# Moving six row products of a recurrence head behind its last level and into its norm's waits

## The reference

```
h = x * (1 + scale1) + shift1
hq, hff, hfb, hi, hg, aq, ak, av, ga, gb = split(h @ w_in)
o_rec = rms_norm(scan_fwd(q, k_f, v, f_f) + scan_bwd(q, k_b, v, f_b)) * silu(hg)   # 8 heads of 128
o_att = attention(rms_norm(aq), rms_norm(ak), av)
x = layer_norm(alpha * x + gate1 * ((sig(ga) * (o_rec @ w_rec) + sig(gb) * (o_att @ w_att)) @ w_out))
# PEER mixer: 128 experts chosen for each token (8 heads x 16), rows of two large tables
a   = gelu(einsum('td,thkd->thk', h2, u_tab[expert]))
out = einsum('thk,thkd->td', gate * a, v_tab[expert])
x = layer_norm(alpha * x + gate2 * out)
```

## Time and profile before

| | |
|---|---|
| runs | 5602.97, 5605.55, 5614.87 us, median 5605.55 us |
| profiled execution, span | 5604.2 us (the page gives no time around the span; the median of the runs is 1.35 us more) |
| PE busy | 4557.5 us, 81% |
| DVE busy | 3712.8 us, 66% |
| POOL busy | 2184.8 us, 39% |
| ACT busy | 1424.7 us, 25% |
| row products of line 1879 | 256, 308.5 us busy, mean 1227 ns |
| latent recurrence heads | some 365 us in each of the two layers |

### The profile page before, as it was taken

One profiled execution on the slowest core, in us unless ns is written; L12 is line 12 of the kernel. 1 busy time (PEld: TensorE's weight loads), 2 busy tenths in 40 slices (PEclk: granted clock), 3 DMA queues, 4 the chain that ended last, 5 costly groups with the idle time before them and its releaser, 6 DMA issues. The chain is left out here.

```text
span 5604.2 us, 60591 instructions
## 1 busy us (share of the span) xinstructions
PE 4557.5 (81%) x17704; PEld 2520.6 (45%) x17704; DVE 3712.8 (66%) x7028; ACT 1424.7 (25%) x3646; POOL 2184.8 (39%) x1826
## 2 busy tenths in 40 slices
PE   7889988888676777777787999888795878777776
PEld 6556655646343322222265566556463433223222
DVE  2357768867788766754532677788677877677545
ACT  2112213411011333333321112134100113333333
POOL 0002124642656454455400121246336554444554
PEclk9999998999888999999999999989897989999999
DMA  7755336785989999999967543457869889999998
GB/s 267 266 184 194 122 131 219 255 331 215 384 318 346 421 419 418 418 421 416 383 225 275 197 163 117 175 191 254 330 243 365 326 311 421 421 419 411 421 421 345
DMA packets 296082, 1703.74 MB, mean 304 GB/s; under 512 B 33360, under 2 KB 43216, under 8 KB 175696
## 3 DMA queue, kind: packets, MB, share of 16 engines
q0 software_dynamic: 258048, 1342.29, 61.3%
q1 hardware_dynamic: 23712, 338.18, 15.8%
q10 hardware_dynamic: 14000, 19.42, 1.0%
HBM read 1694.52 MB, written 5.24 MB: 303 GB/s over the span
## 5 line engine op out<-in xcount | busy, mean ns | idle before, releaser
L368 POOL DMA_INDIRECT arena<-in_peer_uv,eidx x1024 | 1184.3, 1157 | 1458.7 <-POOLq L367 1195.4
L2151 DVE SCALAR_TENSOR_TENSOR arena<-arena 128x1024 f32<-128x1024 f32 x384 | 470.6, 1225 | 349.9 <-DMA arena<-in_peer_uv,eidx 338.4
L861 PE MATMUL banks<-arena 128*128 128x512 f32 x896 | 502.1, 643 | 237.7 <-PEq L1473 234.2
L411 POOL DMA_INDIRECT arena<-in_peer_uv,eidx x384 | 490.3, 1277 | 501.0 <-POOLq L410 475.7
L863 PE MATMUL banks<-arena 128*128 128x512 f32 x896 | 477.8, 616 | 0.0
L834 PE MATMUL banks<-ring,arena 128*128 128x512 f32 x864 | 383.7, 599 | 110.0 <-PEq L816 110.0
L463 ACT ACTIVATE arena<-arena 128x1 f32<-128x1 f32 (+1 forms) x772 | 156.9, 203 | 1035.4 <-ACTq L462 1033.6
L861 PEld LDWEIGHTS banks<-arena 128*128 128x128 f32 x896 | 155.3, 198 | 549.7 <-issue 549.2
L468 ACT ACTIVATE arena<-ident,arena 128x128 f32<-128x128 f32 x832 | 333.6, 401 | 234.7 <-ACTq L467 230.2
L2151 DVE SCALAR_TENSOR_TENSOR ring<-ring,arena 128x1024 f32<-128x1024 f32 x192 | 235.4, 1226 | 211.1 <-DMA ring<-in_peer_uv,eidx 209.9
L2161 DVE SCALAR_TENSOR_TENSOR arena<-arena 128x1024 f32<-128x1024 f32 x256 | 306.9, 1225 | 95.3 <-DMA arena<-in_peer_uv,eidx 80.8
(11 more groups left out here) (303 smaller groups left out, 7763.1 us busy)
## 6 DMA issues: line engine op xcount, KB each, us to landing
ring<-in_wblk SPq DMA_DIRECT2D x160, 2048.0 KB
arena<-in_peer_uv,eidx POOLq DMA_INDIRECT x1408
arena<-in_lnrows ACTq DMA_DIRECT2D x6, 1024.0 KB, 9.5
arena<-in_sk ACTq DMA_DIRECT2D x4, 1024.0 KB, 7.4
hT<-in_peer_uv,eidx POOLq DMA_INDIRECT x192
ring<-in_peer_uv,eidx POOLq DMA_INDIRECT x192
x<-in_x_sample ACTq DMA_DIRECT2D x1, 2048.0 KB, 28.6
out<-arena ACTq DMA_DIRECT2D x4, 512.0 KB, 7.5
```

Of the source, the lines that this page charges most:

```text
L368: nc.gpsimd.indirect_dma_start(grow[j], None, ins["peer_uv"], bass.IndirectOffsetOnAxis(ap=eidx[:, n, r:r + 1].bitcast(U32), axis=0)).then ...
L411: nc.gpsimd.indirect_dma_start(gslot[j], None, ins["peer_uv"].rearrange("(e h) d -> e (h d)", h=2), bass.IndirectOffsetOnAxis(ap=eidx[:, n ...
L861: nc.tensor.matmul(banks[:, b, :], diag[n], row[:, 0:CB], start=start, stop=stop, skip_group_check=True).then_inc(diag_used, 1)
L2151: V.scalar_tensor_tensor(u, u, 1.0, h2[:, t - 2, :], ALU.mult, ALU.mult, accum_out=av[:, r:r + 1])
```

## The change

Only DVE's order changes, in `head`. A head still does six row products. Behind the levels 1, 2, 4, 5 and 6 there is none any more; the one behind the third level (n == 2) stays. Three come behind the last level, after `sc_ready` is signalled and before the wait for the states; one comes after `decays` and ahead of the wait for ACT's squares; and one stands between the signal `var_ready` and the wait for `std_ready`, for which `inverse_root` is written out in place.

```diff
@@ in DVE's head(h), the levels
                         V.tensor_tensor(keep, first, second, ALU.mult)
                         dve.drain()
-                        if n < 6:
-                            ctx_rows(HEAD_ROWS // 6 + (n < HEAD_ROWS % 6))
+                        if n == 2:
+                            ctx_rows(1)
                     dve.drain().then_inc(sc_ready, 1)
+                    ctx_rows(HEAD_ROWS - 3)
                     dve.wait_ge(s0_full, 32)
                     dve.sem_inc(s0_full, -32)
...
                     if more:
                         decays(1 - b, h + 1)
+                    ctx_rows(1)
                     dve.wait_ge(osq_ready, 1)
                     dve.sem_inc(osq_ready, -1)
                     V.tensor_reduce(small[:, 0:LT], r3(osq, P), AX.X, ALU.add)
                     dve.drain()
                     V.tensor_scalar(small[:, 0:LT], small[:, 0:LT], 1.0 / P, EPS, ALU.mult, ALU.add)
-                    inverse_root(LT)
+                    dve.drain().then_inc(var_ready, 1)
+                    ctx_rows(1)
+                    dve.wait_ge(std_ready, 1)
+                    dve.sem_inc(std_ready, -1)
+                    V.reciprocal(small[:, 0:LT], small[:, 0:LT])
+                    dve.drain()
```

## The result

| | before | after |
|---|---|---|
| median of the first series | 5606.09 us (5602.97 to 5614.87, 4 runs) | 5577.88 us (5577.24 to 5584.42, 4 runs) |
| ratio | | 0.995, 95% interval 0.9936 to 0.9965 |
| profiled span | 5604.2 us | 5582.4 us |

The kernel became 28 us faster, where 16 were forecast; 5577.88 lies 2 us under the range of 5580 to 5601. The direction and the mechanism came out, the size did not. The profiled execution of the changed kernel was the slowest of its four (5584.42 us), so its profile shows a smaller lead, 21.8 us by the spans, than the medians do. The changed kernel was measured against before twice more: ratios 0.9952 (0.9939 to 0.9965) and 0.9962 (0.9948 to 0.9976).

What follows compares the result with a forecast made beforehand. DVE was taken to pace the heads' levels. Gains of 10.6 us in middle heads, 3.8 in first heads, 1.5 and 0.1 in last heads made 16.0, taking the span from 5604.2 to 5588.2, median 5590; range 5580 to 5601.

Steps and rivals of the forecast that it cites:

- DVE paces the levels, and PE would be faster: In the heads' levels: DVE sets the 3.74 us step, 1.15 of it the row product; PE alone needs 3.58.
- PE's own pace of 3.58: Levels in heads with a successor: without row products PE sets the step, 3.58 us, read from one place.
- The row product kept behind level 3: In the levels: DVE takes 3.74 there, 0.16 over PE's pace, swallowed by DVE's lead of 0.22 us.
- Rival 1: In the levels: PE's own pace is 3.73, gaining only 5 us, 5601, within no change; chance 0.12.
- the step with the turned output: First of six steps from level 2 in a middle head: PE's pace plus 0.4 for four short passes, 4.0 us.
- Three row products behind the last level at no cost: After the last level: 3.5 us fit inside DVE's 5.79 us wait for the states (3.94 in the last head).
- rival 2: Behind the last level: the three row products wait for gathers and hold the states, making it slower; chance 0.04.
- The row product ahead of the squares: At the norm: delays the next head's second scores 0.48 us in heads with a successor, 1.0 for the last head.
- First heads: First head of each layer, level 2 to the turned keys: 23.39 falls to 21.50 us, a gain of 1.9 each.
- The clock in the last head: Layer 2's last head: half rate eats about 1.4 us of the gain, leaving 1.1 against the norm's 1.0.
- rival 3: Layer 1's last head: PE's clock falls there too, behind a longer wait, costing 1.4 us or more, 5592; chance 0.07.
- I let it pass through whole: Behind the heads: engines meet at a barrier, so the heads' 16.0 us gain reaches the total time whole.

Runs made afterwards that it cites:

- first pair of profiles: One profile each of the kernel before and the changed kernel, from the first series: spans 5604.2 and 5582.4 us, medians 5606.09 and 5577.88 us.
- third profile: The changed kernel run again unaltered, in a series on another chip: 5579.66 us, ratio 0.9962 to the kernel before.
- second profile: The changed kernel run again unaltered for another profile: 5579.15 us, ratio 0.9952 to the kernel before.
- first two series: The changed kernel against the kernel before, measured and then repeated unaltered: 5577.88 us, ratio 0.995, then 5579.15 us, ratio 0.9952.

## Why the prediction was wrong in size and right in its steps

- **DVE paces the levels, and PE would be faster.** Right. With no row product in the heads the steps are PE's 3.47, and where only two levels were emptied only their steps fell, by as much as the norm's rows cost.
- **PE's own pace of 3.58** was mis-sized. I had one place for it, and there the scores had themselves just waited (1.13 long); scores that never wait are 1.05 long and come 3.47 behind the last. The 3.58 were 0.97 for the scores and 2.61 for the projection; the 3.47 are 0.90 and 2.57 (567.08, 567.98 and 570.55 above). The row product kept behind level 3, which I put at nothing, costs 0.18 of it back (3.65). Over the steps a middle head's gain is 1.16 instead of 0.88, and over 12 heads that is 3.4 us. Rival 1, a pace of 3.73, fell. That eight passes of L1217 take 1.13 at most was misread, since the earlier trace rows have 1.49 for a first level; the step with the turned output came at 4.05 for my 4.0 all the same.
- **Three row products behind the last level at no cost.** Right: 2.10 of wait left where I had 2.3; in the last head 0.24 where I had 0.4. No L1879 behind a last level waited for a gather, so rival 2 did not come up. Its price was also counted wrong: the two layers have 14 heads with a successor, not 16.
- **The row product ahead of the squares.** Right in kind, 0.41 against 0.48 in the step from level 1 to 2. In the last head it costs 0.6 (from L1205 to the second scores 7.82 instead of 7.22), where I had 1.0. I started from a sum of squares that was late by itself: before, DVE stood still for 0.43 with nothing to wait for in this head's preparation,

```profile
769.50 0.69 DVE L1962 TENSOR_TENSOR arena<-arena 128x512 f32<-128x512 f32 x1 [0.43 <-issue]
```

  and in the changed kernel it does not.
- **First heads.** 1.9 forecast for each. From level 2 to the turned keys it was 23.39 and is 21.27 in layer 1, and 23.31 and 21.20 in layer 2: 2.1. In layer 2 the first pair of profiles hides it. There the changed kernel's first scores ran behind an idle PE of 3.62, in a stretch with a granted clock of 0.50 (3230 to 3234), and the way to the next scores was 6.58 us; before, the clock was 1.00 (3240 to 3244) and the way 3.55. The other profiles of these two kernels have 5.1 to 5.2 there.
- **The clock in the last head.** The size was nearly right (1.6 for 1.4), the place was not. In my sum layer 2 paid for it and layer 1 did not (rival 3 had it in both). In the changed kernel's first profile neither paid in the levels (21.00 and 20.98 us from the second scores to the turned keys; I had 20.9), and both paid 1.6 later. Busy time by stretch, last head of layer 1, PEclk third from the end:

```profile
795.00:799.00 4.00, 1.60 (x15) 1.44 (x14) 3.10 (x7) 0.00 (x0) 1.66 (x2) 1.00 0.86 262
799.00:803.00 4.00, 4.00 (x21) 3.76 (x20) 0.22 (x2) 0.14 (x1) 0.94 (x1) 0.57 0.63 202
```

  The first line has the clock at its full level, 2.4 GHz; the second is mostly at the lower one, 1.2 GHz. From the outputs to the turned output it is then 11.25 us instead of 9.62. In the third profile of the same kernel the clock fell earlier, behind the longer wait for the second scores:

```profile
764.00:772.00 8.00, 4.33 (x23) 3.05 (x22) 7.07 (x13) 1.49 (x2) 1.87 (x2) 1.00 0.98 375
772.00:776.00 4.00, 4.00 (x12) 2.35 (x11) 2.68 (x6) 0.58 (x1) 0.00 (x0) 0.58 0.10 35
```

  There the levels take 22.3 and the rest is back at 9.62. In the second profile layer 1 pays there (22.36), and layer 2 at both places (22.24 and 11.27). So each last head of the three profiles loses 1.3 to 1.6 once, and one of the six twice. Rival 3 came true in that form, and its loss is inside what the heads gained. The Trainium skill's rule (TensorE: Matmul & The Clock Gate, section HAM oscillation — how this bites in real kernels) that idle gaps bring half rate fits these rows in part. The falls stand behind idle times of PE of 2.40 us (ahead of the outputs at 798.19) and of 3.67 (ahead of the second scores at 771.11 in the third profile). But the kernel before had the same 2.40 ahead of layer 1's outputs, and the changed kernel's first profile had 3.64 ahead of its second scores, and no fall followed either, so the length of one wait does not decide it.
- **"I let it pass through whole."** The step held as far as the runs can tell: 8.6 us added in each layer came out as 17.8 (5597.49 - 5579.66). What failed is what the forecast left out beside it. I built the range from the terms of the heads alone. The heads gained 17.3 us in the first pair of profiles and 19.1 by the means of two of before and three of after: 14.8 in the middle heads (their means went from 44.83 to 43.59; 10.6 forecast), 3.0 in the first ones (3.8) and 1.3 in the last ones (1.6). The medians' leads were 28, 27 and 17. Outside the heads ten profiles of kernels with the same work there show 4867 to 4878 us (before 4878.2 and 4870.1; changed 4873.7, 4877.1 and 4871.6; the others 4866.7 to 4876.5), in no order that goes with the kernel. A median of four or five runs carries that scatter. So of the miss of 12 us, some 3 are PE's pace and other terms of the heads, and the rest I put down to scatter outside them, which is argued and not shown. The profiled executions of the first two series were the slowest of theirs (5584.42 and 5587.23), so no profile shows where the quicker ones were quicker. That the changed kernel also gains a few us outside the heads isn't excluded: the first two intervals begin at a lead of 0.35%, 19.6 us, and reach 0.6%.

## What to carry to other kernels

Before work is moved out of a loop that two engines share, find how fast the other engine goes when nothing holds it: look for a place where it had fallen behind and caught up, and take a pass that did not itself start with a wait, because only the second one shows the whole margin. Filler work belongs into a wait that has room for it and nothing queued behind it that another engine wants; a wait whose signal chain starts behind the filler, such as a sum that a table load follows, is paid for even where the engine seems to have time. And a range needs the scatter of the measurement added to the bounds of the terms: here two profiles of one kernel differ by 7 us.

## What the runs showed of the hardware that was not expected

The same eight passes of scores take 1.13 us when they start behind a wait, even one too short to be printed in the view, and 1.05 right behind other matmuls, and the matmuls behind them begin 0.97 or 0.90 later. That makes two tempos of the same loop, 3.54 and 3.47. And TensorE's clock went to its lower level, 1.2 GHz, in every last head of the three profiles of the changed kernel (granted 0.57 and 0.58 on average over the 4 us shown above). It did so at one of two places, or at both, and which it was differed between runs of the same kernel.
